# Attention kernel: the reciprocal of each softmax row sum moves from the vector engine to GpSimd

## The reference, cut to what matters

```python
# global: every query sees all 1024 keys
sc = jnp.einsum('bqkgd,bskd->bkgqs', qi, k) * scale
p = jax.nn.softmax(sc, axis=-1)
return jnp.einsum('bkgqs,bskd->bqkgd', p, v)
# near: every query sees 8 rows of 16 columns, with a bias by distance
sc = jnp.where(mask, sc + bias, -jnp.inf)
p = jax.nn.softmax(sc, axis=(-2, -1))
```

## Time and profile before

| | us |
|---|---|
| median of three runs | 2451.65 |
| lowest and highest of them | 2449.89, 2452.35 |
| span of the profiled execution | 2449.9 |
| TensorE busy | 2374.6 |
| vector engine busy | 1696.3 |
| ScalarE busy | 1120.4 |
| GpSimd busy | 510.7 |

### The profile page before, as it was taken

How to read it: one execution, slowest core, us unless ns; L and a number is a source line. 1 busy time by engine, 2 the same in 40 slices (tenths; PEclk the granted TensorE clock), 3 DMA queues, 4 the chain that set the end, 5 groups by cost and what they waited for, 6 DMA issues and landing times.

```text
span 2449.9 us, 32619 instructions
## 1 busy us (share of the span) xinstructions
PE 2374.6 (97%) x11129; PEld 1927.6 (79%) x11129; DVE 1696.3 (69%) x2770; ACT 1120.4 (46%) x1950; POOL 510.7 (21%) x447
## 2 busy tenths in 40 slices
PE   7999999899999999999999899999999999998998
PEld 2578888788878888888888788888888897886677
DVE  7788887788786664277766877785641227998863
ACT  3455455444434223245554544343421127887851
POOL 0211001333232000200100333320110003557731
PEclk9999999999999999999999999998999999999999
DMA  8725666654434731235643754430453462336521
GB/s 324 275 84 214 231 219 213 242 169 155 137 99 142 267 111 69 103 106 182 208 173 138 256 190 133 148 127 20 174 140 123 151 185 73 94 96 175 156 69 69
DMA packets 272971, 382.24 MB, mean 156 GB/s; under 512 B 63665, under 2 KB 173361, under 8 KB 272818
## 3 DMA queue, kind: packets, MB, share of 16 engines
q1 hardware_dynamic: 272818, 380.27, 47.5%
HBM read 279.54 MB, written 106.70 MB: 158 GB/s over the span
## 4 chain that ended last, share of the span: by engine, by line
PE 86%; DVE 7%; issue 3%; ACT 2%; POOL 1%; DMA 0%; DVEq 0%; SPq 0%; POOLq 0%; ACTq 0%
PE banks L2793 22%; PE banks L2794 22%; PE banks L2795 22%; PE banks L3339 3%; PE banks L3357 3%; PE banks L2863 2%; PE banks L3326 1%; PE banks L3327 1%; PE banks L3124 1%; PE banks L3125 1%; PE banks L3126 1%; PE banks L2811 1%; DVE stage L2088 1%; DVE X L2462 1%; PE banks L3309 1%
## 5 line engine op out<-in xcount | busy, mean ns | idle before, releaser
L2793 PE MATMUL banks<-Hhi,Whi 128*128 128x512 f32 x1760 | 695.0, 395 | 20.3 <-DVE X L2462 12.5
L2795 PE MATMUL banks<-Hhi,Wlo 128*128 128x512 f32 x1760 | 688.1, 391 | 0.0
L2794 PE MATMUL banks<-Hlo,Whi 128*128 128x512 f32 x1760 | 687.7, 391 | 0.0
L2793 PEld LDWEIGHTS banks<-Hhi,Whi 128*128 128x128 f32 x1760 | 332.0, 189 | 99.2 <-issue 16.1
L2794 PEld LDWEIGHTS banks<-Hlo,Whi 128*128 128x128 f32 x1760 | 332.0, 189 | 70.0 <-issue 2.4
L2795 PEld LDWEIGHTS banks<-Hhi,Wlo 128*128 128x128 f32 x1760 | 331.8, 189 | 69.9
L2793 PE MATMUL banks<-T,Whi 128*128 128x512 f32 x720 | 282.9, 393 | 5.2 <-DVE Wlo L2381 4.9
L2794 PE MATMUL banks<-T,Whi 128*128 128x512 f32 x720 | 282.2, 392 | 0.0
L2795 PE MATMUL banks<-T,Wlo 128*128 128x512 f32 x720 | 282.1, 392 | 0.0
L1722 ACT ACTIVATE Whi<-stage 128x512 fp32r<-128x512 f32 (+2 forms) x186 | 107.7, 579 | 232.0 <-PE banks L2795 231.6
L2462 DVE SCALAR_TENSOR_TENSOR X<-banks,mod,X 128x512 f32<-128x512 f32 x180 | 134.2, 745 | 102.1 <-PE banks L2795 100.8
(11 more groups left out here) (261 smaller groups left out, 4187.6 us busy)
## 6 DMA issues: line engine op xcount, KB each, us to landing
stage<-w SPq DMA_DIRECT2D x58, 1024.0 KB, 6.5
stage<-hidden SPq DMA_DIRECT2D x224, 256.0 KB, 3.5
hidden<-slot SPq DMA_DIRECT2D x196, 256.0 KB, 2.1
stage<-ada_t SPq DMA_DIRECT2D x36, 1024.0 KB, 5.1
x_saved<-X SPq DMA_DIRECT2D x32, 512.0 KB, 4.5
stage<-w_in SPq DMA_DIRECT2D x13, 1024.0 KB, 6.3
stage<-ada_w SPq DMA_DIRECT2D x12, 1024.0 KB, 6.4
X<-x_saved SPq DMA_DIRECT2D x24, 512.0 KB, 5.1
```

The costliest lines, as they stand in the source:

```text
L2793: nc.tensor.matmul(out_bank, whi, xhi, start=start, stop=False, skip_group_check=onto)
L2794: nc.tensor.matmul(out_bank, whi, xlo, start=False, stop=False, skip_group_check=onto)
L2795: return nc.tensor.matmul(out_bank, wlo, xhi, start=False, stop=stop, skip_group_check=onto)
```

## The change

The vector engine's `invert_sum` goes away, with its five places in the order. GpSimd's `scale` computes the reciprocal itself, as a `tensor_tensor` with the operation `pow`: `den` to the power of a constant -1. The constant is one more memset at the start, which is why `set_ready` counts to 7.

```diff
+    minus_one = sb("minus_one", [P, 1])
...
+                nc.gpsimd.memset(minus_one[:], -1.0).then_inc(set_ready, 1)
...
             def scale(T, u, kind):
 
+                pool.wait_ge(exp_done, T("v", u + 1))
+                at = slice(u % 4, u % 4 + 1)
+                nc.gpsimd.tensor_tensor(rden[:, at], den[:, at], minus_one[:], ALU.pow).then_inc(rd_done, 1)
                 pool.wait_ge(rd_done, T("v", u + 1))
                 pool.sem_inc(sums_seen, 1)
...
-            def invert_sum(T, u):
-
-                dve.wait_ge(exp_done, T("v", u + 1))
-                reach(dve, probs_scaled, T("v", u - 3))
-                nc.vector.reciprocal(rden[:, u % 4:u % 4 + 1], den[:, u % 4:u % 4 + 1]).then_inc(rd_done, 1)
...
             def attend(T, kind, i, before, last):
                 dve.wait_ge(a_free, T("a"))
                 for u in range(PAIR):
-                    if kind == "A":
-                        for w, k in lagged(u, 2, kind, before):
-                            invert_sum(T, w)
                     for w, k in lagged(u, 1, kind, before):
                         row_maxima(T, w, k, width(k, w))
-                    if kind == "B":
-                        for w, k in lagged(u, 2, kind, before):
-                            invert_sum(T, w)
```

More of the change, by code:

```diff
@@ L1359, in start @@
                 nc.gpsimd.memset(epsc[:, 2:3], EPS * EPS).then_inc(set_ready, 1)
+                nc.gpsimd.memset(minus_one[:], -1.0).then_inc(set_ready, 1)
                 nc.gpsimd.memset(PH[:, :, 0:PAD], 0.0).then_inc(set_ready, 1)
                 nc.gpsimd.memset(PS[:, :, 0:PAD], 0.0).then_inc(set_ready, 1)
-                pool.wait_ge(set_ready, 6)
+                pool.wait_ge(set_ready, 7)
                 for g in range(4):
@@ L1624, in deviation @@
             def deviation(T, order, hf, dual=False):
-                act.wait_ge(set_ready, 6)
+                act.wait_ge(set_ready, 7)
                 act.wait_ge(stat_done, T("st", complete(order, hf) if dual else (3 if order in ("pooled", "blocks") else 2) * (hf + 1)))
@@ L2180, in pooled @@
                 group, last = k // 2, PS[:, n % 2, :]
-                dve.wait_ge(set_ready, 6)
+                dve.wait_ge(set_ready, 7)
                 dve.wait_ge(tb_ready, 2 * n + 2)
@@ L2765, in attend_end @@
                 row_maxima(T, -1, "B", width("B", -1))
-                invert_sum(T, -2)
                 probs_lo(T, -4, "B")
                 whole_output(T, -3)
-                invert_sum(T, -1)
                 probs_lo(T, -3, "B")
@@ L2801, in start @@
             def start(T):
-                pe.wait_ge(set_ready, 6)
+                pe.wait_ge(set_ready, 7)
             def stat(T, hf, squares, start, stop, weights=None, order="down"):
```

## The result

The kernel with the power on GpSimd takes 2476.11 us (median of 4 runs, 2473.38 to 2482.45); the kernel before took 2451.27 us beside it (4 runs, 2449.89 to 2452.35). The ratio is 1.0106, interval 1.0094 to 1.0117: 24.8 us slower. The forecast was 12.5 us slower, half of that. The sign and the mechanism in the near half came out; the price of the power and the cost in the global half did not.

A forecast was written before the change was run, and what follows sets the result against it. Global half: TensorE bounds, vector engine nearly full; near half: no engine full, GpSimd setting the pace after the change. 13.5 + 0 - 1 = +12.5 us on the median 2451.65 us gave 2464 us; 8-in-10 range 2446 to 2520 us.

The forecast's parts named there:

- steady part: Global half after its first units: a lighter vector engine gives back at most 2.6 us; with lateness behind gatings, set to 0.
- first units: Start of the global half: the second row maximum no longer waits behind a reciprocal; 1 us gained, bounds 0 and 1.3.
- The first term: Near half: 64 steps cost GpSimd 37.8 us, its reciprocal waits cover 24.3 us, so the half grows by 13.5 us.
- duration D: Time of one 128x1 power on GpSimd, in both halves: taken as 0.35 us, between 0.20 us and a far end.
- The hand-over: On GpSimd, time from the power's end to the start of its scaling: taken as 0.24 us.
- P: What the new step costs GpSimd per unit, power plus wait for its result: 0.59 us, lower end 0.44 us.
- 64 P - 24.3: Near half: cost of 64 steps on GpSimd less its 24.3 us of waits for reciprocals, giving 13.5 us of growth.
- As cheap as an addition: Rival: the power takes 0.20 us, as small additions do, and nothing is seen; +2 us, 2454 us; chance 25%.
- Faster: Rival: in the near half GpSimd's scaling starts up to 0.9 us earlier, once in eight units; -10 us, 2441 us; chance 12%.
- The long routine: Rival: the power is a long software routine on GpSimd, 1.13 us each; +79 us, 2531 us; chance 12%.
- the 0.65 us case: Rival in between: the power takes 0.65 us, like the 128x4 subtraction; +41 us, 2493 us; chance 13%.

The follow-up runs named there:

- the cheap operation: The changed kernel with the power replaced by a multiplication of the same shape and waits, so rows are scaled wrongly: 2450.06 us, ratio 1.0000 to the kernel before.
- kernel with two powers: Kernel before with the power on GpSimd in the near half only, made twice per unit, the second waiting for the first: 2510.82 us, ratio 1.0245.
- the short gating: GpSimd's global-half gating cut from 512 to 64 columns: 2447.71 us with the power in the global half only, 2447.01 us in the kernel before.
- the early start: Kernel before with the vector engine's reciprocal put ahead of the next row maximum in the near half: 2448.63 us, ratio 0.9997.

## Why the forecast was right in kind and wrong in size

**What bounds it.** Right. In the near half GpSimd, not yet full but with little to spare, became the engine that sets the pace; in the global half a lighter vector engine was worth little (3.3 us with the cheap operation; I had written at most 2.6 us for the steady part and 1 us for the first units).

**The two terms that failed.** The sum was 13.5 us for the near half, 0 for the steady part of the global half and -1 for the first units. Measured were 19.7 us and, for the whole global half with its first units, 4.7 us. The first term was too small because the duration D of the power was; the second was set to nothing against my own working. Each is worth about 6 us of the 12 that were missing.

**The duration D, the first step that failed.** I put it at 0.35 us, "nearest to the row of the same shape, with something for the arithmetic of a power". It is 0.549 us. The row of 0.20 us is no neighbour of a power: a product of this shape has 0.19 us, and the power takes 0.36 us more. The other end that I had, 0.65 us, was nearer, and I held it away because its row has four elements. The two ends with nothing between them deserved the middle of them (0.43 us) at least. The measured ratio of the two operations, the power on GpSimd and the reciprocal on the vector engine, is 0.549 / 0.16 = 3.4. I had written that the trace shows no operation of one kind and shape on both engines, and that overlooks one pair: with 64x512 elements an addition took 0.67 us on the vector engine and a product 1.28 us on GpSimd, a ratio of 1.9 (the vector engine read one of its inputs from PSUM, GpSimd none). The Trainium skill's ratio of 1.96 (GPSIMD Engine Reference, section 3) is given for an addition; for a reciprocal of 0.16 us it gives an estimated 0.31 us. The pair of 64x512 agrees with it, 1.9, and the power does not, 3.4.

**The hand-over.** Right in size, 0.21 for 0.24 us. P is then 0.75 us, not 0.59.

**The near half.** The sum 64 P - 24.3 was good. With P = 0.75 us it gives 23.7 us, and 19.7 were measured. GpSimd's idle time shows the rest. Before it was 136.35 - 96.79 = 39.6 us, of which 24.3 for the reciprocal. After it is 156.00 - 130.81 = 25.2 us, of which 13.2 for its own powers. So its remaining idle time fell from 15.3 to 12.0 us, which is 3.3 us of cover that I had not counted, and the list grew by 47.2 us and not by 48.0. The two make up the 4.0 us between the sum and the measurement. I had also said that TensorE's waits for the scaling would grow from 13.6 towards 27 us; the same sum is 49.6 us, and it counts waits twice that lie side by side, as does the 13.6. TensorE's idle time, 10.0 and 29.9 us, is the plain measure. The kernel with two powers confirms the slope of 64, and that with the cheap operation the break: 64 x 0.39 = 25 us brought 1.0 us. A cover of 48.0 - 19.7 = 28.3 us, taken from the one power, fits the other two.

**The global half, the second step that failed.** I had 0 and -1 us and measured +4.7, and not by the size of D alone. My own working had TensorE 0.26 us late behind a gating already with D = 0.35, which 16 times makes 4 us; I then set it to 0 because the exponential "can also move up a little". It didn't help: behind a gating the power starts on the gating's end (0.16 us) and not on the exponential. Measured, the scaling is 0.61 us later there and 0.28 beyond its slack, 16 x 0.28 = 4.5 us, beside 4.7. That this is the place is shown by the short gating, and TensorE's 4.9 us of added waits for the scaling are of this size. That the two numbers meet is in part luck. The freed vector engine gives back 1.2 to 3.3 us in the same half (the short gating's pair, the cheap operation); if the two simply add, the late rows cost 6 to 8 us and not 4.5, and where the rest of that lies is open.

**The first units.** The second row maximum does start behind the first without a wait, as I had said, which answers to the earlier trace rows:

```profile
2038.65 2.36 DVE L2728 TENSOR_REDUCE neg_max<-banks 128x1 f32<-128x1024 f32 x2 [18.98 <-PE banks L3318]
```

and so does the second exponential, at 2041.05. Its worth was 1 us by my sum. From the first exponential to the eighth it is 18.00 us before (2034.01 to 2052.01) and 17.41 us after (2039.91 to 2057.32), so 0.6 us are seen, inside my bounds of 0 and 1.3.

**The rivals.** "As cheap as an addition" was right about the time that this would give: the cheap operation took it to no difference (I had +2 us). "Faster" had its condition wrong, P = 0.75 and not below 0.38 us. Of its mechanism the early start was run, on the vector engine, and there it brought nothing, since that engine then waits for exponentials; with a GpSimd step short enough it stays untested. The long routine and the 0.65 us case are excluded by the duration; the latter was the nearer one. With P = 0.75 us in the forecast's own terms, the near half is 64 x 0.75 - 24.3 = 23.7 us and the global half 16 x (0.75 - 0.33) = 6.7 us, and less 1 us it would have been +29 us; 24.8 were measured. So even the right D errs upward by 5 us, most of it the cover of the near half.

## What to carry to other kernels

Before moving an operation to an engine with idle time, add up its start-to-start cost there, the hand-over included, times its number, and set it against that engine's waits in the very stage. In the near half it was free up to there, and beyond it each microsecond was paid in full. Idle time on the sum is not enough: in the global half GpSimd had 88 of 182 us idle, and 4.9 us were lost all the same, because behind a gating another engine took the result with 0.33 us to spare. So look for the tightest place as well as for the total. The price of a function such as a power can't be taken from a product of the same shape; where the trace has neither, measure it with a few instructions at the kernel's start. An instruction put early into an in-order list to hide a hand-over can wait for something later than what stands behind it, and then it delays work that was ready (15.8 us of such waits here).

## What the runs showed of the hardware

- A power of -1 on GpSimd took 0.55 us for 128x1, 0.70 for 128x2 and 1.01 for 128x4; a product 0.19 to 0.20 us for all three. The first power of an execution took 0.57 us, so no more than 0.02 us was paid once at the start.
- A wait of GpSimd for its own result cost 0.20 to 0.21 us between the power and the scaling, but 0.09 us between two powers (1.19 us for two of 0.55). Ahead of the scaling the wait is an instruction of its own and a semaphore is raised behind it; which of the two makes the difference was not tested.
- In the kernel with two powers the granted clock of TensorE was 0.92 on average in the near half, against 0.99 with one and 1.00 before, and TensorE was idle for 56.9 us of it (196.90 - 140.02), against 30.1 and 10.0. Its busy time for the same 708 matmuls rose from 126 to 140 us. It cost nothing here, since the half grew by no more than GpSimd's list. The first time in this half, the granted clock went from 1.00 (2.4 GHz) to 0.50 (1.2 GHz) at about 2229 us, when TensorE had no matmul busy from 2225 to 2226.4 and again from 2227.6 us on.
